# RWKV inverses by blocks of 16 rows with four product stages, and a reordered linear attention, in a two-layer hybrid trunk kernel

## Chip, cores and metric

One core of one Trainium2 chip. The time is device microseconds (us) for one execution of the whole kernel; smaller is better. The engines are PE (TensorE, matrix products; PEld is its weight load), DVE (VectorE), ACT (ScalarE), POOL (GpSimd) and SP (SyncE, which here only issues DMAs). Everything is fp32; a fp32 product appears in the trace as two PE records.

## What is computed

The reference runs two trunk layers over 128 context and 256 latent tokens (384 columns). Each layer has attention, a gated linear attention (GLA) and an RWKV-7 mixer in both directions, then a merge of the three and a feed-forward part. The change touches the GLA and, above all, the RWKV recurrence:

```python
def rwkv7_scan(r, decay, k, v, a_vec, b_vec, s0):
    def step(s, inp):
        rt, wt, kt, vt, at, bt = inp
        sa = jnp.einsum('bhij,bhj->bhi', s, at)
        s = s * wt[:, :, None, :] + sa[..., None] * bt[:, :, None, :] + vt[..., None] * kt[:, :, None, :]
        return s, jnp.einsum('bhij,bhj->bhi', s, rt)
    ...
    y_f, sr_f = rwkv7_scan(r, dec_f, kd_f, vc, -kk, kk * a_f, sr_f0)
    y_b, sr_b = rwkv7_scan(flip_t(r), flip_t(dec_b), flip_t(kd_b), flip_t(vc),
                           flip_t(-kk), flip_t(kk * a_b), sr_b0)
```

## The kernel before

The kernel is written by hand: each engine has its own program, and semaphores join them. A layer has five phases with a barrier between them: projections (0), attention (1), GLA (2), RWKV (3), merge and feed-forward (4). PE products go into six PSUM banks in turn (`item`, `room`): a product waits until the bank used six items earlier has been emptied by the DVE or the ACT. Two more banks serve **fills**. A fill is work of other parts (projections of the gates, `ada`, branch outputs `po`) that PE does in small steps between the steps of its own phase; `fill(k)` does k steps. How many stand at each place of phase 3 is written in the table `FILLS`, one row for each layer (line 349). Steps that are left over are done at the end of the phase (`finish`). The DVE and the ACT empty the fill banks at fixed points of their programs (`side_work`).

Phase 3 takes the 8 RWKV heads as four head pairs n = 0 to 3 (two heads in the partition halves `hr`), each with two directions d and six chunks of 64 tokens. For each pair:

- `logs`, `keys`, `terms` on the DVE, with `decays` and `exps` on the ACT, make the scaled inputs `ar` and `BT`; `grams` (L843) makes the 64x64 strictly triangular matrices `Nt`.
- The inverse of I minus such a matrix is needed. Its 32x32 diagonal blocks are inverted by forward substitution: the DVE turns them into the layout `W` with a stream transpose (`begin`, L2036), the POOL works through 30 rows in 60 dependent operations (L1209, L1211), and the DVE turns the result back twice (`inverses`, L2041 and L2043) and lays it into `ZZ` (L2049).
- `merges` (L856) fills in the block between the diagonal ones by two product stages of 24 small products each: G1 (L863), an ACT copy, G2 (L874, L875), ACT copies into `ZZ`. For the pairs n = 1 and 2 the products of `factors` (MT, BK, VT) and of `turned` (AT, RV) stand between and behind them.
- `transitions` (L949) makes five kinds of `chunkwise` products (WZ, VZ, RT, FT, GG; L946, 24 products each kind), `scan_step` runs the recurrence over the chunks in three steps, and `outputs` makes y.

PE and the DVE go through the pairs in program order. The DVE's order within the round of pair n is: `reads` and `keys`, `transitions`, `terms`, `scan_step` 0 and 1, `logs`, `scan_step` 2, `keys`, `terms`, `grams(n + 2)`, `inverses(n + 1)`; `inverses` waits for the POOL. Before round 0 stands an opening: keys of all heads, head pair 0 and 1's terms, `factors(0)`, `grams(1)` and `inverses(0)`. Below, the time at which WZ of pair n starts on PE is called **T0 to T3**.

Phase 2 (GLA) starts with a chain of decays: z on PE, copies on the ACT (L1413), absolute value on the DVE (L1863), Exp and Ln on the ACT (L1418, L1420), sums on the DVE (L1871 and on), exponentials on the ACT, scaled keys on the DVE (L1893), whose transposes PE waits for (khT, L508). Fourteen distance levels follow (L807), then the outputs `ob` of four heads (L818, L822) and a normalisation, whose last operation is L1967 on the DVE.

## Time and profile before

| what | us |
|---|---|
| median of 3 runs | 2164.12 (2162.21 to 2166.35) |
| the profiled execution | 2163.82 |
| its span, first to last instruction | 2162.0 |
| PE busy | 1946.2 |
| DVE busy | 1020.3 |
| ACT busy | 829.5 |
| POOL busy | 309.5 |

Busy times are unions of the instructions of an engine. Phase 2 stands at 332 to 456 us in layer 0 and 1390.6 to 1515.3 in layer 1; phase 3 at 456 to 742.1 and 1515.3 to 1786. The two phases are repeated nearly alike in the two layers, but layer 0 has more fill work in phase 3.

### The profile page before, as it was taken

How to read it: one execution, taken by the hardware profiler on the slowest of the kernel's cores; microseconds unless marked ns; L12 is line 12 of the kernel's file. 1: busy time of each engine (PE TensorE's matmuls, PEld its weight loads, DVE VectorE, ACT ScalarE, POOL GpSimd, SP SyncE). 2: the span in 40 equal slices, each digit the busy share in tenths (PEclk: the TensorE clock that was granted, in tenths of full speed). 3: DMA queues.
4: the chain of work that ended last, by engine and by line, in shares of the span. 5: the costliest groups of instructions: out<-in, count | busy, mean ns of one | idle time of the engine just before them, and what ended most of it. 6: DMA issues, size and time to landing. Idle time of an engine off the chain costs nothing. (4 is left out here: it accounts for less than half of the span.)

```text
span 2162.0 us, 35730 instructions
## 1 busy us (share of the span) xinstructions
PE 1946.2 (90%) x15251; PEld 1580.7 (73%) x15251; DVE 1020.3 (47%) x1683; ACT 829.5 (38%) x1340; POOL 309.5 (14%) x549
## 2 busy tenths in 40 slices
PE   6899998988689898999989989989786898899998
PEld 3799444655476698999979974546455768899998
DVE  0435425856663454433332454186766545434332
ACT  2433535343353335333253335333433344533321
POOL 2000000007772000000000000000377600000000
PEclk9999999998899999999999999999988899999999
DMA  6543332322103333443434433332200023344442
GB/s 226 175 120 107 104 115 81 97 73 89 50 3 99 129 119 85 131 123 104 131 107 119 127 104 96 105 102 92 70 21 2 3 65 121 97 133 119 116 121 83
DMA packets 267924, 214.31 MB, mean 99 GB/s; under 512 B 7225, under 2 KB 259544, under 8 KB 267512
## 3 DMA queue, kind: packets, MB, share of 16 engines
q1 hardware_dynamic: 264816, 204.43, 31.3%
q0 software_dynamic: 2736, 7.54, 1.1%
q8 instruction: 122, 2.00, 0.4%
q14 instruction: 34, 0.28, 0.0%
q10 hardware_dynamic: 216, 0.06, 0.0%
HBM read 209.13 MB, written 2.88 MB: 98 GB/s over the span
## 5 line engine op out<-in xcount | busy, mean ns | idle before, releaser
L550 PE MATMUL bank<-scr_rounded 128*128 128x384 f32 (+1 forms) x1312 | 444.1, 338 | 0.0
L548 PE MATMUL bank<-scr_rounded 128*128 128x384 f32 x672 | 232.4, 346 | 37.1 <-DVE scr_rounded L1716 35.6
L604 PE MATMUL bank<-h,ring 128*128 128x384 f32 x640 | 238.1, 517 | 29.1 <-DVE gtmp L1703 10.9
L550 PEld LDWEIGHTS bank<-scr_rounded 128*128 128x128 f32 (+1 forms) x1312 | 249.4, 190 | 1.0
L549 PE MATMUL bank<-scr_rounded 128*128 128x384 f32 x672 | 230.4, 343 | 0.0
L1711 DVE TENSOR_TENSOR scr_rounded<-ring,scr_rounded 128x2048 fp32r<-128x2048 f32 (+1 forms) x64 | 136.1, 2126 | 188.4 <-ACT scr_rounded L1266 187.6
L548 PE MATMUL bank<-scr_rounded,gate_rounded 128*128 128x384 f32 (+1 forms) x640 | 214.1, 335 | 4.4 <-DVE scr_rounded L1711 4.4
L549 PE MATMUL bank<-scr_rounded,gate_rounded 128*128 128x384 f32 (+1 forms) x640 | 213.9, 334 | 0.0
L604 PEld LDWEIGHTS bank<-h,ring 128*128 128x128 f32 x640 | 121.2, 198 | 114.8 <-issue 43.4
L599 PE MATMUL bank<-ring,scond 128*2 128x256 f32 x768 | 175.4, 381 | 8.3 <-DVEq L343 5.0
L1711 DVE TENSOR_TENSOR scr_rounded<-ring,gate_rounded 128x2048 fp32r<-128x2048 f32 (+3 forms) x64 | 130.2, 2034 | 104.6 <-ACT gate_rounded L1266 104.0
L1266 ACT ACTIVATE scr_rounded<-ring 128x2048 fp32r<-128x2048 f32 (+1 forms) x64 | 114.0, 1781 | 152.7 <-PE bank L550 75.2
L1266 ACT ACTIVATE gate_rounded<-ring 128x2048 fp32r<-128x2048 f32 (+3 forms) x64 | 109.3, 1707 | 146.5 <-PE bank L550 85.8
L548 PEld LDWEIGHTS bank<-scr_rounded 128*128 128x128 f32 x672 | 130.9, 195 | 42.4 <-issue 38.6
L1211 POOL TENSOR_TENSOR cst<-cst,lora 128x30 f32<-128x30 f32 (+14 forms) x240 | 142.9, 596 | 18.8
L599 PEld LDWEIGHTS bank<-ring,scond 128*2 128x2 f32 x768 | 61.7, 85 | 109.3 <-issue 21.2
L1209 POOL TENSOR_TENSOR lora<-cst 128x30 f32<-128x30 f32 (+14 forms) x240 | 131.9, 550 | 18.2
L549 PEld LDWEIGHTS bank<-scr_rounded 128*128 128x128 f32 x672 | 131.0, 195 | 0.0
L548 PEld LDWEIGHTS bank<-scr_rounded,gate_rounded 128*128 128x128 f32 (+1 forms) x640 | 118.9, 186 | 5.9 <-DVE scr_rounded L1711 5.0
L549 PEld LDWEIGHTS bank<-scr_rounded,gate_rounded 128*128 128x128 f32 (+1 forms) x640 | 118.9, 186 | 1.0
L2241 DVE TENSOR_TENSOR arena<-bank,arena 128x384 f32<-128x384 f32 x44 | 24.5, 558 | 176.7 <-PE bank L550 173.7
L610 PE MATMUL bank<-arena,ring 128*128 128x384 f32 x256 | 90.6, 496 | 4.2 <-DVE gtmp L1703 1.9
(369 smaller groups left out, 3250.1 us busy)
## 6 DMA issues: line engine op xcount, KB each, us to landing
ring<-in_w_in_dram SPq DMA_DIRECT2D x56, 1024.0 KB, 5.3
ring<-in_w_ada_dram SPq DMA_DIRECT2D x48, 1024.0 KB, 5.2
ring<-in_w_ffn_in_dram SPq DMA_DIRECT2D x88, 512.0 KB, 5.1
ring<-in_w_ffn_out_dram SPq DMA_DIRECT2D x32, 704.0 KB, 4.6
ring<-in_w_out_dram SPq DMA_DIRECT2D x8, 1024.0 KB, 5.3
ring<-in_w_po_a_dram SPq DMA_DIRECT2D x4, 1024.0 KB, 6.6
ring<-in_w_po_b_dram SPq DMA_DIRECT2D x4, 1024.0 KB, 5.9
ring<-in_w_po_c_dram SPq DMA_DIRECT2D x4, 1024.0 KB, 5.1
```

What stands on the lines that cost most here:

```text
L548: pe.matmul(o, w_hi[:, k, :], right[0][k], start=k == 0, stop=False)
L549: pe.matmul(o, w_hi[:, k, :], right[1][k], start=False, stop=False)
L550: ins = pe.matmul(o, w_lo[:, k, :], right[0][k], start=False, stop=k == nk - 1)
L599: ins = pe.matmul(b[0:2, 0:256], scond[:, :, k], w[:, k, :], start=k == 0, stop=k == KD - 1)
L604: ins = pe.matmul(b[:, 0:T], w[:, k, 128 * (j % 2):128 * (j % 2) + 128], h[:, k, :], start=k == 0, stop=k == KD - 1)
L610: ins = pe.matmul(b[:, 0:T], w[:, k, 128 * (j % 4):128 * (j % 4) + 128], src[:, k, :], start=k == 0, stop=k == 3)
L1209: gp.tensor_tensor(t, W[:, i + 1:32, i:i + 1].to_broadcast([128, more, i]), over(W[:, i, 0:i], more), mult).then_inc(*step())
L1211: gp.tensor_tensor(W[:, i + 1:32, 0:i], W[:, i + 1:32, 0:i], t, add).then_inc(*(step() if i < 30 else tells("rw_inv")))
L1266: A(shaped(whi[m % 2], name, j), weights(l, name, j), ACT.Copy).then_inc(*tells("w_hi"))
L1711: tt(shaped(wlo[m % 2], name, j), weights(l, name, j), value(shaped(whi[m % 2], name, j)), sub).then_inc(*tells("w_lo"))
L2241: tt(ff[:, j, :], b[:, 0:T], ff[:, j, :], mult).then_inc(*empties("ffi", l, j, 1))
```

## The change

1. **Blocks of 16.** The DVE compresses twice, so that the diagonal blocks are 16x16 (`own`, then `Cc` of 512 columns in place of 1024). `begin` transposes 512 columns. The POOL's 60 operations are gone. `substitution(rows)` on the DVE does rows 1 to 14 in 28 dependent operations of 28 to 112 elements for a partition. For pair 0 it stands in the opening, behind `begin(0)`; for later pairs it is cut into rows 1 to 5, 6 to 10 and 11 to 14, behind `scan_step` 0, 1 and 2.
2. **Four product stages.** With D the inverse of the diagonal blocks and N the part off them, PE makes MM and QQ, then SS, EE and FF, each by `chunkwise`, 24 products for each of the five kinds. ACT copies MM; the DVE copies QQ and adds after SS, EE and FF. The POOL only masks N (`off_blocks`) and lays out the second form of D (`own_blocks`).
3. **Order.** `factors` is split into `factor(n, d)` and `values(n)`, `turned` into `turned` (AT) and `read` (RV); for n = 1 and 2 these stand between the stages. For n = 0 and 3 there are three places for fills in a merge, not one. `FILLS` is new: in layer 0 the steps up to T0 go from 29 to 19, in layer 1 from 27 to 19; the sums of the rows go from 56 to 56 and from 47 to 44. `finish` does what is left.
4. **GLA.** On the ACT the squares of the RWKV keys stand behind Exp and Ln. PE has `fill(4)` before the products of those squares, and `fill(6)` in place of `fill(4)` behind them. The DVE empties only the first two fills before L1871. The `ob` products with `att` are done for all heads first, then those with the states, with the two partition halves in turn.

```diff
-        FILLS = ((4, 6, 2, 4, 4, 4, 2, 2, 1, 1, 1, 1, 1, 2, 1, 1, 1, 1, 2, 1, 1, 1, 2, 2, 2, 2, 1, 1, 1, 1),
-                 (4, 6, 2, 4, 4, 2, 2, 2, 1, 1, 1, 1, 1, 0, 1, 1, 1, 1, 0, 1, 1, 1, 1, 2, 1, 1, 1, 1, 1, 1))
+        FILLS = ((4, 6, 2, 1, 1, 1, 1, 0, 1, 1, 1, 2, 2, 2, 1, 1, 3, 2, 2, 1, 1, 3, 2, 2, 1, 1, 1, 1, 1, 1, 1, 2, 2, 2),
+                 (4, 6, 2, 1, 1, 1, 1, 0, 1, 1, 1, 1, 1, 1, 1, 1, 2, 1, 1, 1, 1, 2, 1, 1, 1, 1, 1, 1, 1, 1, 1, 1, 1, 1))
...
+                    for d in range(2):
+                        chunkwise("MM", "A", n, d, lambda h, c: Zt[d][hr[h], c, :], lambda h, c: Nt[n % 2][hr[h], d, c, :])
+                        chunkwise("QQ", "V", n, d, lambda h, c: Nt[n % 2][hr[h], d, c, :], lambda h, c: Zt[d][hr[h], c, :])
                     if n in (1, 2):
-                        factors(n)
+                        factor(n, 0)
                     else:
                         fill(next(steps))
...
+                        chunkwise("SS", "V", n, d, lambda h, c: Mm[hr[h], d, c, :], lambda h, c: Qm[hr[h], d, c, :])
+                    if n in (1, 2):
+                        factor(n, 1)
+                    else:
+                        fill(next(steps))
...
+                        chunkwise("EE", "V", n, d, lambda h, c: Mm[hr[h], d, c, :], lambda h, c: Sm[d][hr[h], c, :])
...
+                        chunkwise("FF", "V", n, d, lambda h, c: pair[0][hr[h], c, :], lambda h, c: pair[1][hr[h], c, :])
...
+                def substitution(rows):
+
+                    for i in rows:
+                        more = 15 - i
+                        t = term[:, 0:2 * more * i].rearrange("p (j a k) -> p j a k", j=more, a=2)
+                        tt(t, W[:, i + 1:16, :, i:i + 1].to_broadcast([128, more, 2, i]),
+                           W[:, i, :, 0:i].unsqueeze(1).to_broadcast([128, more, 2, i]), mult).then_inc(*step())
+                        dve.wait_ge(*last())
+                        tt(W[:, i + 1:16, :, 0:i], W[:, i + 1:16, :, 0:i], t, add).then_inc(*step())
+                        dve.wait_ge(*last())
...
                     scan_step(n, 0)
+                    if n < 3:
+                        substitution(range(1, 6))
                     scan_step(n, 1)
+                    if n < 3:
+                        substitution(range(6, 11))
...
                     scan_step(n, 2)
+                    if n < 3:
+                        substitution(range(11, 15))
...
-                for hp in range(4):
-                    A(kkn[hp], pc[:, 4 + hp, :], ACT.Square, scale=P(l, "k_k", hp)).then_inc(*tells("rw_kksq"))
                 act.wait_ge(S["gla_abs"], told("gla_abs", l, 1))
...
                 A(lg, lg, ACT.Ln, bias=1.0).then_inc(*tells("gla_log"))
+                for hp in range(4):
+                    A(kkn[hp], pc[:, 4 + hp, :], ACT.Square, scale=P(l, "k_k", hp)).then_inc(*tells("rw_kksq"))
...
+                        pe.matmul(outs_b[hh][:, cs], vbt[:, cc, 128 * hh:128 * hh + 128], att[:, hh, cs], start=cc == 0, stop=cc == 0,
+                                  skip_group_check=True)
+                for hp in range(2):
+                    for cc in range(1, C):
+                        cs = slice(CH * cc, CH * cc + CH)
+                        for d in range(2):
+                            st = s0 if cc == first[d] else s1
+                            for half, r in enumerate(hr):
+                                ins = pe.matmul(outs_b[2 * hp + half][:, cs], st[r, d, hp, :], qe[r, 2 * d + hp, cs], start=False, stop=d == 1,
+                                                skip_group_check=True)
+                    ins.then_inc(psum_ready, 2)
```

PE, phase 3 of layer 0, the merge of pair 1 before. L604 is a fill, L863 is G1, L893 to L916 `factors`, L874 and L875 G2:

```order
L604 MATMUL bank<-h,ring 128x384 x2
L863 MATMUL bank<-scr,cst 32x32 x24
L893 MATMUL bank<-scr 64x128 x12
L508 MATMUL bank<-cst,scr 128x64 x6
L893 MATMUL bank<-scr 64x128 x12
L905 MATMUL bank<-cst,scr 64x64 x12
...
L508 MATMUL bank<-cst,arena 128x128 x3
L916 MATMUL bank<-cst,arena 64x128 x6
L874 MATMUL bank<-scr 32x32
L875 MATMUL bank<-scr 32x32
```

The same place in the changed kernel. L975 is `chunkwise` (twice 12 rows of MM and QQ for each direction, then SS, EE and FF), L915 and L927 are `factor`, L953 AT, L966 RV, L942 the values:

```order
L975 MATMUL bank<-cst,scr 64x64 x12
L975 MATMUL bank<-scr,cst 64x64 x12
...
L915 MATMUL bank<-scr 64x128 x12
L927 MATMUL bank<-cst,scr 64x64 x12
L975 MATMUL bank<-scr,cst 64x64 x24
...
L975 MATMUL bank<-lora,cst 64x64 x12
L975 MATMUL bank<-cst 64x64 x12
...
L942 MATMUL bank<-cst,arena 64x128 x6
L953 MATMUL bank<-cst,scr 64x64 x24
L975 MATMUL bank<-scr,lora 64x64 x12
L975 MATMUL bank<-cst,scr 64x64 x12
L966 MATMUL bank<-arena,gate 64x64 x24
```

The 48 products of 32x32 have become 120 of 64x64, and `factor` and AT stand between the stages. On the DVE, the `inverses` of pair 0 before (L1980 to L1984 are `logs`, L2041 to L2049 the turning back, L2036 `begin` of pair 1, L2064 `reads`):

```order
L1980 SCALAR_TENSOR_TENSOR scr<-cst,arena 128x384
L1982 TENSOR_TENSOR scr<-scr 128x384
L1984 TENSOR_TENSOR scr<-scr,arena 128x384
L2041 STREAM_TRANSPOSE scr<-cst 128x32x32
L2043 STREAM_TRANSPOSE scr<-cst 128x32x32
L2036 STREAM_TRANSPOSE cst<-cst 128x1024
L2049 TENSOR_TENSOR scr<-scr,cst 128x384 x2
L1696 TENSOR_TENSOR mod<-bank,par 128x4
L2064 TENSOR_TENSOR scr<-bank,scr 128x384 x2
```

And in the changed kernel, with L2105 to L2089 the turning back and `begin`, L2160 to L2170 the evictions of QQ, SS, EE and FF:

```order
L2031 TENSOR_TENSOR scr<-scr,arena 128x384
L2105 STREAM_TRANSPOSE scr<-cst 128x16x32
L2110 TENSOR_TENSOR scr<-scr,cst 128x384 x2
L2114 STREAM_TRANSPOSE scr<-cst 128x16x32
L2085 STREAM_TRANSPOSE cst<-cst 128x512
L2089 MEMSET cst 128x16 x2
L2160 COPY scr<-bank 128x384 x2
L2164 TENSOR_TENSOR lora<-bank,scr 128x384
L2164 TENSOR_TENSOR cst<-bank,scr 128x384
...
L2170 TENSOR_TENSOR scr<-bank,scr 128x384 x2
L2129 TENSOR_TENSOR scr<-bank,scr 128x384 x2
```

The DVE no longer waits for the POOL there, and has eight evictions more. Between the scan steps of round 0 (L2149) now stands the substitution (L2097 multiplies, L2100 adds):

```order
L2097 TENSOR_TENSOR lora<-cst 128x100
L2100 TENSOR_TENSOR cst<-cst,lora 128x20x5
L2149 SCALAR_TENSOR_TENSOR scr<-bank,small,scr 128x64 x2
L2097 TENSOR_TENSOR lora<-cst 128x108
L2100 TENSOR_TENSOR cst<-cst,lora 128x18x6
```

Each of the ten operations behind scan step 1 (the last two rows are its first ones) now runs before `logs` and scan step 2 on the DVE.

## Rows read from the trace of the kernel before

**Rows 1.** The page: span, and first row of its busy times.

```profile
span 2162.0 us, 35730 instructions
...
PE 1946.2 (90%) x15251; PEld 1580.7 (73%) x15251; DVE 1020.3 (47%) x1683; ACT 829.5 (38%) x1340; POOL 309.5 (14%) x549
```

**Rows 2.** Windows by stage: length; PE, PEld, DVE, ACT, POOL busy; clock; DMA share, GB/s.

```profile
332.00:456.00 124.00, 112.56 (x736) 69.12 (x737) 84.38 (x164) 51.96 (x79) 1.52 (x2) 0.96 0.31 98
456.00:542.30 86.30, 69.83 (x623) 41.71 (x623) 55.91 (x91) 34.22 (x63) 44.49 (x78) 0.86 0.25 77
542.30:599.90 57.60, 41.44 (x821) 30.76 (x822) 37.36 (x63) 21.23 (x43) 46.34 (x79) 0.88 0.12 39
599.90:644.20 44.30, 37.16 (x809) 29.67 (x804) 31.46 (x57) 21.02 (x43) 29.98 (x56) 0.92 0.01 3
644.20:700.90 56.70, 55.05 (x845) 35.98 (x841) 20.64 (x41) 23.03 (x47) 18.81 (x36) 1.00 0.30 94
700.90:742.10 41.20, 37.89 (x448) 25.48 (x448) 12.81 (x29) 11.31 (x18) 0.87 (x1) 1.00 0.20 59
...
1515.30:1601.10 85.80, 65.98 (x593) 40.94 (x593) 56.86 (x92) 33.44 (x61) 44.63 (x78) 0.86 0.17 53
1601.10:1655.40 54.30, 39.38 (x795) 31.22 (x796) 36.51 (x58) 21.18 (x42) 43.35 (x74) 0.81 0.01 2
1655.40:1704.10 48.70, 36.82 (x800) 29.82 (x794) 32.79 (x57) 19.23 (x41) 34.28 (x62) 0.82 0.01 2
1704.10:1754.80 50.70, 47.47 (x804) 34.26 (x799) 20.60 (x39) 23.70 (x46) 17.28 (x34) 1.00 0.15 44
1754.80:1786.00 31.20, 29.10 (x412) 21.48 (x412) 12.53 (x27) 10.45 (x16) 0.87 (x1) 0.95 0.16 44
```

**Rows 3.** Timeline of PE, layer 0: start, us, group, idle before and its releaser.

```profile
510.50 1.56 PE L893 MATMUL bank<-scr 64*64 64x128 f32 x24 [8.64 <-DVE gate L2101]
...
584.07 2.90 PE L604 MATMUL bank<-h,ring 128*128 128x384 f32 x4 [10.88 <-DVE gtmp L1703]
```

**Rows 4.** PE's waits in total: us, times, longest.

```profile
PE bank L863 <- DVE scr L2049: 27.0, 4, 11.0
```

**Rows 5.** Who waited for the POOL's substitution: us, times.

```profile
  DVE scr L2041: 11.5, 4
```

**Rows 6.** Timeline of PE: G1, a fill step, WZ and VZ together (48 products).

```profile
537.48 0.95 PE L863 MATMUL bank<-scr,arena 32*32 32x32 f32 x48
...
542.25 3.02 PE L946 MATMUL bank<-scr 64*64 64x64 f32 x96 [1.45 <-ACT scr L1569]
...
564.49 1.56 PE L610 MATMUL bank<-arena,ring 128*128 128x384 f32 x4
```

**Rows 7.** Timeline of the DVE: small operations without and with POOL at work, transpose, eviction.

```profile
463.78 0.16 DVE L2009 TENSOR_TENSOR small<-small 128x5 f32<-128x5 f32 x1
...
494.12 0.41 DVE L2009 TENSOR_TENSOR small<-small 128x5 f32<-128x5 f32 x1
...
624.91 1.92 DVE L2041 STREAM_TRANSPOSE scr<-cst 128x1024 f32<-128x1024 f32 x1
...
647.94 1.26 DVE L2064 TENSOR_TENSOR scr<-bank,scr 128x384 f32<-128x384 f32 x2 [7.12 <-PE bank L946]
```

**Rows 8.** Timeline of all engines, phase 2 of layer 0.

```profile
341.62 1.48 ACT L1420 ACTIVATE scr<-scr 128x1536 f32<-128x1536 f32 x1
...
345.20 1.75 DVE L1871 SCALAR_TENSOR_TENSOR scr<-scr 128x1536 f32<-128x1536 f32 x1
...
360.38 1.97 PE L508 MATMUL bank<-cst,scr 128*128 128x128 f32 x8 [9.22 <-DVE scr L1893]
...
431.63 1.61 PE L807 MATMUL bank<-scr 64*128 64x128 f32 x24
...
439.70 0.71 PE L822 MATMUL bank<-scr 64*128 64x128 f32 x4
...
453.09 0.56 DVE L1967 TENSOR_TENSOR arena<-arena 128x384 f32<-128x384 f32 x1
```

More of the change, by code:

```diff
@@ new lines, in merges @@
+                    if n in (1, 2):
+                        values(n)
+                        turned(n)
+                    else:
+                        fill(next(steps))
+                    pe.wait_ge(S["rw_zn"], told("rw_zn", l, n + 1))
+                    for d in range(2):
+                        pe.wait_ge(*emptied("EE", l, n, d))
+                        pair = (Sm[0], Zn[0]) if d == 0 else (Zn[1], Sm[1])
+                        chunkwise("FF", "V", n, d, lambda h, c: pair[0][hr[h], c, :], lambda h, c: pair[1][hr[h], c, :])
@@ L1050, in _ @@
                 turned(0)
+                read(0)
                 fill(next(steps))
@@ L1071, in _ @@
                         fill(next(steps))
-                        factors(3)
+                        factor(3, 0)
+                        factor(3, 1)
+                        values(3)
                         fill(next(steps))
                         turned(3)
+                        read(3)
                         fill(next(steps))
@@ L1602, in _ @@
                 exps(3)
-                factors(0)
+                factor(0, 0)
+                factor(0, 1)
+                values(0)
                 decays(4)
                 turned(0)
+                read(0)
                 for n in range(4):
@@ L1616, in _ @@
                     if n == 2:
-                        factors(3)
+                        factor(3, 0)
+                        factor(3, 1)
+                        values(3)
                         turned(3)
+                        read(3)
                     if n == 2:
@@ L2032, in grams @@
                     dve.wait_ge(*last())
                 def begin(n):
-                    dve.transpose(W, Cc).then_inc(*tells("rw_w"))
+                    dve.transpose(W.rearrange("p j a i -> p j (a i)"), Cc).then_inc(*step())
+                    dve.wait_ge(*last())
+                    flat = W.rearrange("p j a i -> p (j a i)")
+                    for a in range(2):
+                        dve.memset(flat[:, 16 * a:512:33], 1.0).then_inc(*step())
+                    dve.wait_ge(*last())
@@ L2044, in inverses @@
+                    ins.then_inc(*tells("rw_zt"))
+                    dve.transpose(Zc.rearrange("p u j -> p j u"), W.rearrange("p j a i -> p j (a i)")).then_inc(*tells("rw_zc"))
                     dve.wait_ge(*last())
@@ L2090, in scan_step, with merges @@
                                 op0=mult, op1=add).then_inc(*empties("H", l, n, s, d))
-                def factors(n):
-                    i, hp = n % 2, n
-                    for d in range(2):
-                        for j in range(2):
-                            for h in range(2):
-                                side_work("MT", l, n, d, j, h)
-                                dve.wait_ge(psum_ready, filled("MT", l, n, d, j, h))
-                                b = bank("MT", l, n, d, j, h)
-                                tt(MMt[:, d, h, 3 * j:3 * j + 3, :], c3(b[:, 0:T]), over(seen[:, d, :], 3), mult).then_inc(*empties("MT", l, n, d, j, h))
-                    for d in range(2):
-                        c = scanned(d, 0)[1]
-                        ts(HS[:, d, c, :], h0[:, 4 * d + hp, :], es[i][d][:, 0, c:c + 1], None, mult).then_inc(*tells("rw_h"))
+                def merges(n):
+                    for d in range(2):
+                        cp(Qm[:, d, :, :], taken("QQ", n, d)).then_inc(*empties("QQ", l, n, d))
+                    if n in (1, 2):
+                        factor(n, 0)
+                    for d in range(2):
+                        tt(Sm[d], taken("SS", n, d), Qm[:, d, :, :], add).then_inc(*empties("SS", l, n, d))
+                    if n in (1, 2):
+                        factor(n, 1)
+                    for d in range(2):
+                        tt(Sm[d], taken("EE", n, d), Qm[:, d, :, :], add).then_inc(*empties("EE", l, n, d))
+                    for d in range(2):
+                        tt(ZZ[:, d, :, :], taken("FF", n, d), ZZ[:, d, :, :], add).then_inc(*empties("FF", l, n, d))
@@ new lines, in factor @@
+                def factor(n, d):
+                    i, hp = n % 2, n
+                    for j in range(2):
+                        for h in range(2):
+                            side_work("MT", l, n, d, j, h)
+                            dve.wait_ge(psum_ready, filled("MT", l, n, d, j, h))
+                            b = bank("MT", l, n, d, j, h)
+                            tt(MMt[:, d, h, 3 * j:3 * j + 3, :], c3(b[:, 0:T]), over(seen[:, d, :], 3), mult).then_inc(*empties("MT", l, n, d, j, h))
+                    if d:
+                        for e in range(2):
+                            c = scanned(e, 0)[1]
+                            ts(HS[:, e, c, :], h0[:, 4 * e + hp, :], es[i][e][:, 0, c:c + 1], None, mult).then_inc(*tells("rw_h"))
@@ L2147, in _ @@
                 begin(0)
+                substitution(range(1, 15))
                 for g in (2, 3):
@@ L2158, in _ @@
                         logs(6)
[L2159 to L2160 removed]
+                    merges(n)
                     reads(n)
```

236 lines of the change are left out of this document (116 added, 120 removed).

## The prediction

> **What bounds the kernel now.** I read the busy shares first: PE is busy for 1946 of 2162 us, the DVE for less than half, the POOL for a seventh [rows 1]. So PE's order of work is the path, and a change pays where PE stands still or where its work shrinks. Then the windows of the two phases touched [rows 2]. In phase 3 of layer 0 (286 us) PE is busy 70, 41, 37, 55 and 38 us in the opening and the rounds of pairs 0 to 3. 45 us are idle, nearly all before T2; round 2 is full (55.05 of 56.7 us). In layer 1 (271 us) 52 us are idle. The granted clock says that idle time costs twice: it is 0.81 to 0.92 in the stages with stalls and 1.00 in round 2, so behind stalls PE works at 1.2 GHz in place of 2.4 GHz. In window terms (1 - clock) x length, for example 0.14 x 86.3 = 12 us in the opening, is the time at full clock that was lost there.
>
> Which stalls? In the opening PE waits 8.6 us for the eviction of MT, because the DVE is still in the terms of pair 1; in round 0 it waits 10.9 us in a fill whose bank the DVE empties late, behind the inverses [rows 3]. G1 waits for `ZZ` 27 us in four places [rows 4]. But the DVE waited for the POOL only 11.5 us in four places in the whole kernel [rows 5]: the POOL's 41 us for an inverse are mostly hidden. What it costs beside that is contention. A DVE operation of 5 elements takes 0.16 us when the POOL rests and 0.41 us when it works [rows 7].
>
> **Part 1, the substitution.** 28 dependent operations of 28 to 112 elements, 2240 in all. From the row of 5 elements 0.16 us [rows 7], from an eviction of two times 384 elements 1.26 us, 0.63 for each [rows 7]: a fixed part near 0.16 and about 1.2 ns for an element. 28 x 0.16 + 2240 x 0.0012 = 7.2 us; with a few hundredths for each dependence I take **8 us** an inverse. Bounds: 28 x 0.16 = 4.5 us below and 28 x 0.41 = 11.5 us above, the row with contention. I stay near the lower row since the POOL now has only three short operations for a pair.
>
> The row says that a small operation is nearly all fixed cost. The Trainium skill, VectorE: DVE Perf Modes, section on the TRN2 errata, says the same in kind and speaks against cutting work into small operations; its table gives 58 cycles and one for each element at 0.96 GHz. By that table, an estimate, an inverse would be 28 x 60 ns + 2.3 = 4.0 us, and the six inverses behind the opening and the first loops would make the sum some 20 us smaller; I go by the row.
>
> **Part 2, the DVE's path in a round.** From T0 to G1's input before: 571.7 - 542.3 = 29 us of evictions, keys, terms and `grams`, then POOL wait, two transposes of 1.92 us [rows 7], one for the next pair and the layout, 39 us in sum. After: the same 29 us less 6 us (some 15 operations of 384 elements fall from about 0.9 to 0.56 us as the contention of rows 7 goes) plus 8 us for the substitution, 1.5 us for the second compression, and half a transpose and the layout, 2 us: 33.5 us in round 0 and 33 in round 1, where before it was 39 and 31. So the DVE is earlier by 5 us in round 0 and later by 2 in round 1. It is this path that PE waits for, not a POOL.
>
> **Part 3, the merge on PE.** WZ and VZ, 48 products of 64x64, take 3.02 us [rows 6], so 24 take 1.5 us, and five kinds take 7.5 us. G1 takes 0.95 us [rows 6] and G2 about 0.5. **+6 us for each pair**, 48 us of PE for the 8 pairs. The stages themselves: in each, the DVE needs 0.63 us for a direction while PE does the other, so with `factor` or a fill between them there is little wait. A merge that had 4.8 us from G1 to T0 (with one fill step and 1.45 us of waiting, rows 6) becomes 3.0 + 1.5 + 1.5 + 1.5 + 0.7 and three steps of 1.5 to 1.9 us: 13.5 us. In rounds 0 and 1 with `factor`, AT, RV and VT in it: 3 + 4.5 + 3.3 x 2 + 1.5 + 1.5 + 1.5 = 18.6 us behind the DVE's signal, 20 in round 0 where `logs` delays the first eviction.
>
> **Part 4, stage by stage** (before from rows 2).
> - Opening, 86 us. The DVE has 8 us more and 6 less contention before it empties MT, so PE leaves its stall about 1 us later; `ZZ` is ready 8 us earlier, and the merge is 9 us longer: **+0.5**. But 10 fill steps (8 in layer 1) of about 1.5 us [rows 6] have left the opening and must be done later: PE stands idle for some 35 us there in place of 17.
> - Round 0: 33.6 + 20 = **54 us** against 57.6 and 54.3. The stall of 10.9 us goes, but its place is taken by the merge.
> - Round 1: 33 + 18.6 = **51.5 us** against 44.3 and 48.7.
> - Round 2: PE is full, so all work adds: 56.7 + 8.9 for the merge of pair 3 with its two more fill steps = **66 us**, and 50.7 + 7.3 = **58 us**.
> - Round 3: three fill steps more, 4.4 us, less a little stall: **45 us** against 41.2, and **35 us** against 31.2.
>
> Layer 0: 86.5 + 54 + 51.5 + 66 + 45 = 303 against 286, **+17 us**. Layer 1: 86.5 + 54 + 51.5 + 58 + 35 = 285 against 271, **+14 us**.
>
> **Part 5, GLA.** Here I see a gain. Ln ends at 343.1, but L1871 starts at 345.2, since the DVE first empties fills; and Exp starts behind the four squares and a table load, 1.3 us after it could [rows 8]. Both go: the scaled keys are 2.8 us earlier, and so is khT. PE waits 9.2 us there [rows 8], and two fill steps more fit into the wait. The 16 state products of `ob` take 0.71 us for each two (four records), 5.6 us; when two partition halves alternate, as in L807, 24 records take 1.6 us [rows 8], so 32 take 2.1: 3.2 us less of PE, and 2.6 less on the way to the last L1967, which ends at 453.7 [rows 8]. The phase ends at 456.0 because PE then has two `ada` fills left; one of them has moved to the front. New end about 451.3 - 2.8: **-7.5 us a layer**, -15 in all. If the tail doesn't follow, only the 2.8 at the front and 2.2 of the tail remain, -10; nothing makes it a loss.
>
> **Sum.** 17 + 14 - 15 = +16 us on 2163.8 of the profiled execution (0.3 below the median of the runs), so **2180 us**.
>
> **Rivals.**
> - *PE's work alone sets the rounds.* If the DVE's path is shorter than I sum it (substitution at 4.5 us, evictions under PE), the rounds shrink to PE's work at full clock. Layer 0 behind the opening: 286 - 86 = 200 us, less 28 idle and some 8 of clock, plus 18 of merges and 15 of fills: 197, so -2 with the opening. Layer 1: 185, less 31 and 18, plus 18 and 12: 166, so -18; I allow it -10 with the stalls that its few fills leave. With GLA: -27, **2137 us**; halfway, 2150. For it: the DVE is busy only 31 of 44 us in round 1. Against it: those are dependent steps, and 8 us are added to them. It decides from a substitution under 5 us.
> - *The two parts cancel.* The rounds cost half of what I say, **2164 us**.
> - *The GLA part doesn't act*, because the fill work moved forward is missed by no one and the DVE's tail holds the end: +31 less 2, **2193 us**.
> - *The substitution runs at the row with contention*, 11.5 us: 3.5 us more in three places a layer, **2201 us**. For it: `W` is read in short runs, and the POOL masks at that time.
>
> **Numbers.** Forecast (2170 to 2190) 0.52; PE's work alone 0.24; cancelling 0.12; GLA without effect 0.07; slow substitution 0.05. Measurement tells apart about 0.2%, 4 us. Faster 0.25, same 0.13, slower 0.62. The range takes in half of the first rival and the last but one: 2147 to 2196 us.
>
> **What would show it.** In the changed profile: L2097 and L2100 at 0.2 to 0.3 us each and 8 us an inverse; L975 at 1.5 us for 24 products; T1 - T0 near 54, T2 - T1 near 51; PE idle over 30 us in the opening; round 2 at 66 and 58 us with clock 1.00; phase 2 at 116 to 118 us. I am wrong if the opening is shorter by over 5 us, or if rounds 0 and 1 are under 50 us.

## The result, and the profile after it

The changed kernel takes **2175.81 us** (median of 7 runs, 2173.01 to 2179.07); the kernel before, in the same rounds, 2166.35 us (2162.21 to 2170.43). The ratio is 1.0046, with a 95% interval of 1.0031 to 1.0061: **slower by 9.5 us**. The interval leaves out 1, but the difference is under half a percent. The forecast was 2180 us.

The page of the changed kernel, its first rows, as in [rows 1]:

```profile
span 2176.9 us, 37908 instructions
...
PE 1974.6 (91%) x16403; PEld 1608.5 (74%) x16403; DVE 1064.2 (49%) x1995; ACT 820.0 (38%) x1308; POOL 58.4 (3%) x85
```

PE is busy for 28 us more, the DVE for 44 us more, and 251 us of the POOL's work are gone. Which stage pays, the windows show. They have the columns of [rows 2]; the first six are phase 2, the opening and the rounds 0 to 3 of layer 0, the others the same of layer 1:

```profile
335.16:447.48 112.32, 105.18 (x737) 63.97 (x737) 84.02 (x164) 51.35 (x79) 1.52 (x2) 1.00 0.35 114
447.48:536.59 89.11, 64.36 (x703) 43.33 (x703) 58.56 (x129) 31.64 (x56) 6.00 (x6) 0.79 0.03 8
536.59:586.85 50.26, 45.36 (x964) 34.75 (x964) 40.47 (x100) 20.96 (x40) 3.17 (x3) 1.00 0.26 86
586.85:646.80 59.95, 49.93 (x989) 36.55 (x987) 38.71 (x100) 19.44 (x40) 3.17 (x3) 0.91 0.17 55
646.80:711.03 64.23, 62.27 (x991) 43.71 (x987) 30.46 (x77) 23.09 (x43) 1.70 (x2) 1.00 0.17 52
711.03:757.84 46.81, 43.44 (x476) 27.78 (x474) 13.53 (x31) 11.69 (x19) 0.87 (x1) 1.00 0.32 95
1407.29:1519.61 112.32, 105.18 (x737) 63.97 (x737) 84.02 (x164) 51.40 (x79) 1.52 (x2) 1.00 0.36 115
1519.61:1608.49 88.88, 64.14 (x704) 43.28 (x704) 58.56 (x129) 31.64 (x56) 6.00 (x6) 0.79 0.03 8
1608.49:1658.80 50.31, 41.71 (x941) 34.09 (x941) 40.48 (x100) 20.40 (x39) 3.17 (x3) 0.97 0.20 65
1658.80:1708.55 49.75, 41.51 (x951) 34.42 (x949) 38.09 (x96) 20.10 (x39) 3.17 (x3) 0.97 0.01 3
1708.55:1769.32 60.77, 56.64 (x962) 41.61 (x956) 30.31 (x76) 20.47 (x39) 1.70 (x2) 1.00 0.12 37
1769.32:1802.41 33.09, 31.65 (x426) 22.14 (x424) 13.08 (x28) 12.23 (x18) 0.87 (x1) 1.00 0.15 41
```

Against [rows 2]:

| stage | layer 0: before, after, forecast | layer 1: before, after, forecast |
|---|---|---|
| phase 2 | 124.0, 112.3, 116.5 | 124.7, 112.3, 117 |
| opening | 86.3, 89.1, 86.5 | 85.8, 88.9, 86.5 |
| round 0 | 57.6, 50.3, 54 | 54.3, 50.3, 54 |
| round 1 | 44.3, 60.0, 51.5 | 48.7, 49.8, 51.5 |
| round 2 | 56.7, 64.2, 66 | 50.7, 60.8, 58 |
| round 3 | 41.2, 46.8, 45 | 31.2, 33.1, 35 |

Phase 2 gives back 24 us in sum; phase 3 costs 24 us in layer 0 and 12 in layer 1. The remaining 3 us of the profiled span lie ahead of phase 2 of layer 0, where the code is the same; in the runs below phase 2 of layer 0 starts anywhere from 331.6 to 334.8 us, here at 335.2, so I don't put them down to the change.

Three readings behind the table. First, the substitution on the DVE; the groups (busy time, mean ns of one) and operations of round 0 of layer 0:

```profile
L2097 DVE TENSOR_TENSOR lora<-cst 128x28 f32<-128x28 f32 (+6 forms) x112 | 27.9, 249 | 3.2
L2100 DVE TENSOR_TENSOR cst<-cst,lora 128x28 f32<-128x28 f32 (+6 forms) x112 | 27.3, 244 | 3.9
...
549.34 0.21 DVE L2100 TENSOR_TENSOR cst<-cst,lora 128x28 f32<-128x28 f32 x1
...
553.09 0.28 DVE L2100 TENSOR_TENSOR cst<-cst,lora 128x112 f32<-128x112 f32 x1
```

224 operations at 0.25 us, and 0.03 to 0.05 us between them: 8 inverses of 8 us, on a chain of the DVE at whose end PE waits.

Second, stalls: PE's two in the opening of layer 0, and in its round 1 two of PE and one of the ACT (columns of [rows 3]):

```profile
494.33 1.56 PE L915 MATMUL bank<-scr 64*64 64x128 f32 x24 [12.20 <-ACT arena L1523]
...
503.87 1.56 PE L915 MATMUL bank<-scr 64*64 64x128 f32 x24 [6.70 <-DVE gate L2180]
...
598.41 5.30 PE L606 MATMUL bank<-ring,scond 128*2 128x256 f32 x16 [2.17 <-ACT modrow L1294]
...
615.55 4.58 PE L617 MATMUL bank<-arena,ring 128*128 128x384 f32 x8 [5.02 <-ACT modrow L1294]
...
613.45 0.21 ACT L1537 ACTIVATE small<-scr 128x6 f32<-128x6 f32 x1 [5.51 <-DVE scr L2031]
```

The single stall of 8.64 us at MT has become 19 us in two pieces: few fills are left to stand there. In round 1 the fills wait twice for a bank that the ACT empties late, once within the three steps in front of scan step 0 and once behind scan step 2, and what stands behind the waits runs more slowly: 5.30 us for 16 records of L606 that take 3.62 us elsewhere, 4.58 us for 8 of L617 that take 2.82 us at the upper clock level (2.4 GHz). The second wait goes back to the DVE: ten operations of the substitution stand ahead of `logs` (L2031), the ACT waits 5.51 us for `logs`, and only behind the exponentials does it empty the bank.

Third, phase 2, where [rows 8] showed khT behind 9.22 us of idleness:

```profile
360.68 1.09 PE L515 MATMUL bank<-cst,scr 128*128 128x128 f32 x8 [2.42 <-DVE scr L1940]
361.70 1.97 PE L800 MATMUL bank<-gate,scr 128*64 128x128 f32 x32
...
433.72 2.06 PE L833 MATMUL bank<-scr 64*128 64x128 f32 x32
```

### The profile page after: what moved, and what is told of

Its sections match the earlier page's. It is cut to its first block, busy times and chain, and to the rows that moved or that the text cites. A ratio compares the mean times of both kernels' runs of the same rounds, so it can differ in the third digit from the quotient of the medians.

```text
span 2176.9 us, 37908 instructions
## 1 busy us (share of the span) xinstructions
PE 1974.6 (91%) x16403; PEld 1608.5 (74%) x16403; DVE 1064.2 (49%) x1995; ACT 820.0 (38%) x1308; POOL 58.4 (3%) x85
## 4 chain that ended last, share of the span: by engine, by line
PE 74%; DVE 12%; ACT 8%; issue 2%; DMA 1%; PEldq 1%; PEld 0%; ACTq 0%; POOL 0%; DVEq 0%; SPq 0%; POOLq 0%
PE bank L555 11%; PE bank L557 11%; PE bank L556 11%; PE bank L611 7%; PE bank L606 6%; PE bank L975 5%; PE bank L1159 3%; PE bank L1161 3%; PE bank L1160 3%; PE bank L617 2%; PE bank L515 2%; PE bank L814 2%; ACT h L1324 1%; DVE cst L2100 1%; DVE lora L2097 1%
## 5 line engine op out<-in xcount | busy, mean ns | idle before, releaser
L611 PE MATMUL bank<-h,ring 128*128 128x384 f32 x640 | 232.7, 507 | 14.2 <-ACT gtmp L1307 8.0
L606 PE MATMUL bank<-ring,scond 128*2 128x256 f32 x768 | 180.0, 388 | 9.7 <-DVEq L350 5.0
L606 PEld LDWEIGHTS bank<-ring,scond 128*2 128x2 f32 x768 | 62.5, 86 | 114.9 <-issue 29.9
L617 PE MATMUL bank<-arena,ring 128*128 128x384 f32 x256 | 96.1, 519 | 11.9 <-DVEq L350 5.3
L617 PEld LDWEIGHTS bank<-arena,ring 128*128 128x128 f32 x256 | 48.5, 198 | 43.9 <-issue 17.8
L915 PE MATMUL bank<-scr 64*64 64x128 f32 x768 | 33.5, 304 | 38.7 <-ACT arena L1523 24.4
```

The costliest lines, as they stand in the source:

```text
L606: ins = pe.matmul(b[0:2, 0:256], scond[:, :, k], w[:, k, :], start=k == 0, stop=k == KD - 1)
L611: ins = pe.matmul(b[:, 0:T], w[:, k, 128 * (j % 2):128 * (j % 2) + 128], h[:, k, :], start=k == 0, stop=k == KD - 1)
L617: ins = pe.matmul(b[:, 0:T], w[:, k, 128 * (j % 4):128 * (j % 4) + 128], src[:, k, :], start=k == 0, stop=k == 3)
```

## Experiments

Each run is given by its ratio to the kernel before on the same chip; the changed kernel stands at 1.0046. A hundredth is 21.7 us.

### The two parts apart

The GLA part alone, on the kernel before, and the RWKV part alone:

```diff
-                fill(4)
+                fill(6)
...
-                for hp in range(4):
-                    A(kkn[hp], pc[:, 4 + hp, :], ACT.Square, scale=P(l, "k_k", hp)).then_inc(*tells("rw_kksq"))
                 act.wait_ge(S["gla_abs"], told("gla_abs", l, 1))
```

> The kernel before with the GLA part of the change alone (ACT squares behind Exp and Ln, fill(4) ahead of and fill(6) behind the products of the squares, the DVE's later fill evictions, the regrouped ob products); the inverses are the old ones. Theory W (the windows of the changed kernel are the whole of it: phase 2 takes 112.3 us there in place of 124.0 and 124.7, and nothing comes back later): 24 us less than the kernel before, near 2142 us. Theory P (the prediction's terms, 7.5 us a layer): near 2151 us. Theory N (the gain in phase 2 needs the new phase 3, or is given back by the fill work that phase 3 no longer finds): 2160 us or more.

Measured: **2143.39 us** (2142.88 to 2145.68), ratio 0.9904 (0.9891 to 0.9918), 21 us less. Both phases 2 have the length of the changed kernel:

```profile
334.12:446.42 112.30, 105.18 (x737) 63.97 (x737) 83.98 (x164) 51.33 (x79) 1.52 (x2) 1.00 0.36 115
```

> The changed kernel with the GLA part put back as it was; only the inverses, their order and the table of fills are new. If the two parts are independent, this is the changed kernel plus what the GLA part gives: near 2200 us by the windows (phase 3 is 24 us longer in layer 0 and 12 in layer 1), near 2191 us by the prediction's 15 us. If they are not independent, the sum of this run's difference and that of the GLA part alone differs from the difference of the changed kernel (about +10 us) by more than 4 us.

Measured: **2197.0 us** (2196.21 to 2198.08), ratio 1.015 (1.0136 to 1.0164), 33 us more. -21 and +33 make +12; the changed kernel is at about +10. Within the noise the parts are independent, and theories P and N of the first run are out: P is 8 us off, N 17.

The front of the GLA part alone, on the kernel before (order on the ACT, fills and their evictions, but the old `ob` products):

> The kernel before with only the front of the GLA part (ACT squares behind Exp and Ln, fill(4) and fill(6), the DVE's later fill evictions); the ob products stay as they were. Together with the ob products the gain was 21 us. By the windows of the changed kernel, khT starts 2.8 us earlier, and no stall of 9.2 us stands ahead of it, so that the 32 products behind it take 1.97 us in place of 3.68; one ada step has left the end. I expect 5.5 to 8 us a layer from the front and 4 from the tail: 2149 to 2155 us. Rival (the tail holds the end of the phase, as the prediction had it, so the front alone gives only 2.8 us a layer): 2158 us or more.

Measured: **2153.0 us** (2151.92 to 2156.23), ratio 0.9944 (0.9928 to 0.9961), 12 to 14 us less. So the front gives some 6.5 us a layer and the tail 4 to 5. The rival, 2.8 us a layer, falls.

### What the substitution costs on the DVE

```diff
                     scan_step(n, 0)
-                    if n < 3:
-                        substitution(range(1, 6))
                     scan_step(n, 1)
-                    if n < 3:
-                        substitution(range(6, 11))
...
                     scan_step(n, 2)
-                    if n < 3:
-                        substitution(range(11, 15))
```

> The changed kernel without the substitution behind the scan steps (pairs 1 to 3 get wrong inverses; pair 0 keeps its own); the DVE's path is 8 us shorter in each round, PE's work is the same. Theory D (the DVE's path sets rounds 0 and 1): each of these four rounds shrinks until PE's own work fills it, that is by 5 us in layer 0 and by 8 in layer 1 (PE is busy 45.4 of 50.3 us in round 0, 41.6 of 50 us in layer 1), in sum 20 to 26 us less than the changed kernel, near 2153 us; round 2 stays. Rival PE (PE's own work sets the rounds and the DVE is waited for only at its edges): less than 6 us, 2170 us or more.

Measured: 2147.17 us (2146.13 to 2151.1), ratio 0.9924 (0.9911 to 0.9938): **26 us less than the changed kernel**. Rounds 0 and 1 of layer 1, which were 50.31 and 49.75 us:

```profile
1593.30:1636.30 43.00, 40.02 (x941) 32.71 (x941) 33.65 (x72) 20.39 (x39) 3.17 (x3) 1.00 0.23 76
1636.30:1679.30 43.00, 39.64 (x951) 32.71 (x949) 31.41 (x68) 20.10 (x39) 3.17 (x3) 1.00 0.01 3
```

7 of 8 us come back from each, PE's busy time falls by 2 us with the clock at its upper level throughout, and round 2 gives 2 to 3.5 us. In layer 0, which has more fills, round 0 falls only from 50.26 to 46.45 us, where PE is then busy for 44.95, and round 1 from 59.95 to 53.30. The DVE's chain sets these rounds as the change left them; the rival, that PE's own work sets them, falls, though in round 0 of layer 0 PE's work is the next limit, after 4 us.

Its place: all 28 operations in one piece behind scan step 2.

> The changed kernel with all 28 operations of a substitution in one piece behind scan step 2, not cut in three behind the three scan steps. Theory L (the DVE's path is one chain, and its length does not depend on the place): within 4 us of the changed kernel, 2172 to 2180 us. Rival W (the pieces behind scan steps 0 and 1 stand partly in time that the DVE waits for the next scan product of PE, so late ones cost more): 2 to 3 us in each of the four rounds 0 and 1, 2184 us or more. Rival Q (the pieces delay the scan's next step, so together behind it they cost less): 2168 us or less.

Measured: 2181.63 us (2180.3 to 2182.81), ratio 1.0073 (1.0058 to 1.0088), some 6 us above the changed kernel, between theory L and rival W; the intervals of the two ratios touch. What is late then are the keys and terms of the next pair, in round 0 and, through a fill's bank, in round 1:

```profile
562.03 1.55 PE L865 MATMUL bank<-scr 64*64 64x64 f32 x24 [4.32 <-DVE scr L2063]
...
623.86 2.90 PE L611 MATMUL bank<-h,ring 128*128 128x384 f32 x4 [7.39 <-DVE gtmp L1749]
```

Cutting it in three is worth a little; where it stands is not what costs most. But its place decides one wait. The fill behind scan step 2 in round 1 of layer 0, which waited 5.02 us for the ACT, in the run without the substitution and then in this one:

```profile
605.35 2.82 PE L617 MATMUL bank<-arena,ring 128*128 128x384 f32 x8 [0.45 <-ACT modrow L1294]
...
610.59 2.82 PE L617 MATMUL bank<-arena,ring 128*128 128x384 f32 x8 [0.46 <-ACT modrow L1294]
```

Both have the changed kernel's table of fills. So this wait is not one of too many fills alone; it is the substitution's, since it holds up `logs` and with it the ACT. The first wait stays, at 1.81 us in both (2.17 in the changed kernel).

### One product stage

```diff
-                    for d in range(2):
-                        pe.wait_ge(*emptied("SS", l, n, d))
-                        chunkwise("EE", "V", n, d, lambda h, c: Mm[hr[h], d, c, :], lambda h, c: Sm[d][hr[h], c, :])
...
-                    for d in range(2):
-                        tt(Sm[d], taken("EE", n, d), Qm[:, d, :, :], add).then_inc(*empties("EE", l, n, d))
```

> The changed kernel without the stage EE (24 products of 64x64 for a pair and two DVE additions; the inverses are incomplete). Theory M (a stage lies on the path from the DVE's transposes to T, in all 8 merges; 1.5 us of PE and, where no work is left to stand between, some of the DVE's additions): 1.5 to 2 us for each pair, 12 to 16 us less than the changed kernel, 2160 to 2164 us. Rival S (the stages hide in other stalls): under 8 us, 2168 us or more.

Measured: 2164.84 us (2161.95 to 2169.84), ratio 0.9997 (0.9983 to 1.0012): 11 us less than the changed kernel, 1.3 us for each of 8 merges. Theory M is a little high, rival S too low. The 24 products are 1.5 us of PE, so a stage costs about its products and no long wait.

### The fills that left the opening

```diff
-        FILLS = ((4, 6, 2, 1, 1, 1, 1, 0, 1, 1, 1, 2, 2, 2, 1, 1, 3, 2, 2, 1, 1, 3, 2, 2, 1, ...
+        FILLS = ((4, 6, 2, 4, 4, 4, 2, 0, 1, 1, 1, 1, 1, 1, 1, 1, 1, 1, 1, 1, 1, 2, 1, 1, 1, ...
```

The row of layer 1 changes in the same way: seven steps more in its opening, fewer in rounds 1 to 3.

> The changed kernel with another table of fills: in layer 0 ten steps more in the opening (places 4 to 7: 4, 4, 4, 2 in place of 1, 1, 1, 1) and ten fewer in rounds 0 to 2; in layer 1 seven more in the opening and some fewer at the end. Theory F (PE stands idle for 25 us in each opening, and waits there for the DVE, so fills are free there, while round 2 is full and round 1 of layer 0 waits 7 us for the ACT in its three bunched fills): opening unchanged within 3 us, layer 0 shorter by 10 to 15 us, layer 1 by 5, in sum 2158 to 2164 us. Theory D (the fills push MT and with it the whole chain of the opening): the opening grows by what the rounds lose, 2173 to 2180 us.

Measured: **2157.63 us** (2155.21 to 2162.01), ratio 0.9972 (0.9961 to 0.9983): 16 us less than the changed kernel, and less than the kernel before. Opening, rounds 0 to 2 of layer 0:

```profile
446.71:535.27 88.56, 74.59 (x765) 45.49 (x765) 60.49 (x132) 33.19 (x59) 6.70 (x6) 0.90 0.20 67
535.27:587.70 52.43, 45.38 (x979) 36.57 (x979) 40.75 (x103) 20.85 (x41) 3.17 (x3) 0.93 0.14 43
587.70:636.30 48.60, 40.03 (x925) 33.26 (x924) 37.06 (x94) 19.85 (x38) 3.16 (x3) 0.96 0.01 3
636.30:698.10 61.80, 58.40 (x979) 41.42 (x975) 30.57 (x77) 21.27 (x41) 1.70 (x2) 1.00 0.18 55
```

The opening takes ten more steps in 0.5 us less: they stood in waiting time. Round 1, with four steps fewer (6.2 us) and without the waits for the ACT, falls from 59.95 to 48.60; the run doesn't part the two. Round 0 shows the other side: with three steps fewer it is 2.2 us longer. PE is busy as long as before (45.38 us) at a clock of 0.93, and stands idle for 7.1 us in place of 4.9, the longest time (3.46 us) before the outputs (L1024). Theory F holds.

### What the POOL's substitution had cost

The kernel before, with 58 of the 60 POOL operations of each inverse left out:

```diff
-                    for i in range(1, 31):
+                    for i in range(30, 31):
```

> The kernel before with 58 of the 60 POOL operations of each substitution left out (the inverses are wrong; PE, ACT and DVE do what they did). It prices what the change took away. Theory C (the POOL was mostly hidden but slowed the DVE: 6 us of contention in each of some six stages, and 11.5 us of waits): 25 to 40 us less than the kernel before, 2125 to 2140 us, with 384-element DVE operations at 0.55 us throughout. Rival H (hidden work costs nothing): at most the 11.5 us that the DVE waited, 2153 us or more.

Measured: **2110.11 us** (2106.88 to 2120.79), ratio 0.9748 (0.9714 to 0.9782): 47 to 62 us less, more than theory C. Opening and round 0 of layer 0, then of layer 1:

```profile
457.76:537.99 80.23, 69.04 (x621) 41.24 (x622) 50.19 (x91) 34.26 (x63) 4.12 (x8) 0.89 0.26 82
537.99:587.10 49.11, 41.74 (x820) 31.32 (x821) 31.10 (x63) 21.21 (x43) 0.92 (x3) 0.86 0.15 45
...
1500.39:1573.70 73.31, 61.87 (x593) 38.41 (x593) 51.05 (x92) 33.49 (x61) 4.14 (x8) 0.91 0.20 62
1573.70:1615.50 41.80, 35.20 (x795) 28.42 (x796) 29.53 (x58) 21.21 (x42) 0.92 (x3) 0.92 0.01 2
```

They were 86.3, 57.6, 85.8 and 54.3 us (the profile is of the slowest of the four executions, 10 us above the median). The DVE's busy time in them falls by 5.7, 6.3, 5.8 and 7.0 us, the contention that the prediction priced at 6. But the stages fall by 6, 8.5, 12.5 and 12.5 us. What can add to the contention is the wait in `inverses` and the clock behind the stalls (0.86, 0.88, 0.86 and 0.81 before, 0.89, 0.86, 0.91 and 0.92 here); their shares were not measured apart. The POOL, busy 14% of the span and waited for 11.5 us, cost some 50.

Which operations contend? The kernel before, round 0 of layer 0, the POOL at work; the last row is the changed kernel, where the POOL rests:

```profile
549.68 1.01 DVE L2070 TENSOR_TENSOR scr<-bank,cst 128x384 f32<-128x384 f32 x2
...
551.72 1.05 POOL L1211 TENSOR_TENSOR cst<-cst,lora 128x238 f32<-128x238 f32 x1
...
552.18 1.01 DVE L2005 TENSOR_TENSOR scr<-scr,arena 128x384 f32<-128x384 f32 x1
...
554.00 0.60 DVE L2009 TENSOR_TENSOR small<-small 128x5 f32<-128x5 f32 x1
...
545.49 0.55 DVE L2052 TENSOR_TENSOR scr<-scr,arena 128x384 f32<-128x384 f32 x1
```

The first row is two operations in 1.01 us, with one input in PSUM (`bank`), as long as the same two take in the changed kernel. L2005 is one operation with both inputs in SBUF, the memory of the tiles that are not banks: 1.01 us, where the changed kernel has 0.55. The POOL suffers too: its operation in the second row takes 1.05 us, and the same one of 238 elements takes 0.65 at 557.00. The Trainium skill, SBUF — State Buffer, section "SBUF: two separate sides", says so: a DVE operation with two SBUF inputs and a POOL operation that reads SBUF exclude each other for a whole instruction. The rows agree: both engines' operations with SBUF inputs grow, the DVE's with a PSUM input don't.

### The same 28 operations on the POOL

If the POOL cost 50 us because 41 us of its work reached over the DVE's keys and terms, a short chain that stands beside the merge, where the DVE takes from PSUM, should cost next to nothing. (The expectation on record is more careful; it allows up to 10 us of contention.)

```diff
+                def substitution(n):
+
+                    gp.wait_ge(S["rw_w"], told("rw_w", l, n + 1))
+                    for i in range(1, 15):
...
                     own_blocks(n)
+                    if n < 3:
+                        substitution(n + 1)
...
                 def inverses(n):
 
+                    dve.wait_ge(S["rw_inv"], told("rw_inv", l, n + 1))
```

> The changed kernel with the same 28 operations of each substitution moved from the DVE to the POOL (all four pairs), in one piece behind begin; everything else as in the changed kernel. Leaving the substitution out gave 2147 us. The POOL needs about 14 us for it (operations of 58 to 108 elements took 0.39 to 0.46 us on the POOL before), of some 45 us that it has. Theory V (the DVE's 8 us are the cost, contention is smaller): 2147 plus up to 10 us of contention, minus the 8 us of pair 0 in each opening that are saved too: 2140 to 2157 us. Rival K (contention and the hand-over cost as much as the move saves, as the change seems to assume): 2165 us or more.

Measured: **2133.7 us** (2133.18 to 2137.32), ratio 0.9853 (0.9825 to 0.9881), 42 us less than the changed kernel; the time lies below the expected range. Rounds 0 and 1 of layer 1, then the POOL's first and last operation of an inverse and the DVE beside it and behind it (layer 0):

```profile
1581.10:1624.10 43.00, 40.01 (x940) 32.69 (x942) 33.71 (x72) 20.39 (x39) 14.27 (x37) 1.00 0.23 76
1624.10:1667.10 43.00, 39.65 (x951) 32.71 (x949) 31.40 (x68) 20.08 (x39) 13.22 (x33) 1.00 0.01 3
...
520.53 0.28 POOL L1264 TENSOR_TENSOR lora<-cst 128x28 f32<-128x28 f32 x1
...
532.07 0.24 POOL L1267 TENSOR_TENSOR cst<-cst,lora 128x28 f32<-128x28 f32 x1
...
526.21 0.56 DVE L2174 TENSOR_TENSOR lora<-bank,scr 128x384 f32<-128x384 f32 x1 [1.78 <-PE bank L975]
...
538.75 0.55 DVE L2068 TENSOR_TENSOR scr<-scr,arena 128x384 f32<-128x384 f32 x1
...
539.69 0.16 DVE L2072 TENSOR_TENSOR small<-small 128x5 f32<-128x5 f32 x1
```

These rounds have the length that they have with no substitution at all; in layer 0 they differ from it by 0.05 and 0.2 us. The POOL needs 11.8 us beside evictions, and is done before the DVE's keys begin (534.80).

The products of the substitution done three times, so that the POOL works twice as long:

> As pool16 (2133.7 us), with each product of the substitution done three times into the same place, so that the POOL has 56 operations for an inverse, near 26 us in place of 13; nothing else changes. Theory K (the POOL's work costs nothing while it lies beside the merge, where the DVE only evicts, and costs when it reaches the DVE's keys and terms, where a 5-element operation took 0.41 to 0.60 us beside the POOL and 0.16 us without): 10 to 20 us more, 2144 to 2154 us, and 5-element operations of 0.3 us or more in rounds 0 and 1, which are 0.16 us in pool16. Rival H (what cost time before was only the length of the POOL's chain, 41 us, for which the DVE waited in the end): within 4 us of pool16, since 26 us still end long before they are waited for.

Measured: 2138.7 us (2132.28 to 2142.57), ratio 0.9872 (0.9849 to 0.9894): 4 us above pool16, which its interval doesn't separate from zero. The stages say more. Rounds 0 and 1 of layer 1, which were 43.00 each:

```profile
1584.10:1629.50 45.40, 41.57 (x939) 33.36 (x941) 34.68 (x72) 20.40 (x39) 26.57 (x63) 0.96 0.22 72
1629.50:1674.30 44.80, 41.30 (x953) 34.34 (x949) 32.17 (x68) 20.16 (x39) 26.66 (x64) 0.96 0.01 3
```

The DVE is busy 0.8 to 1.0 us longer, its 5-element operation in the first terms of each round takes 0.27 to 0.31 us while the second stays at 0.16, and the rounds grow by 2.4 and 1.8 us. That is theory K's mechanism at a third of its price or less; in layer 0, where more fills fill the rounds, it makes +1.0 and -1.2 us.

With the fill table of the run above:

> As pool16, with the table of fills of the run that moved fill steps into the opening (that gave 18 us on the changed kernel). Theory: the two gains add, since one shortens the DVE's path in the rounds and the other fills idle time in the opening: 12 to 18 us under pool16. Rival: with the DVE out of the opening's path PE has less idle time to fill there, and the rounds are full again: under 8 us. It beats the kernel before with the GLA part alone (2143 us) if it comes under 2139.

Measured: **2114.14 us** (2110.79 to 2115.76), ratio 0.9756 (0.9733 to 0.978), 21 us under pool16, more than the 12 to 18 expected: the gains add. Opening and rounds 0 and 1 of layer 0:

```profile
444.18:530.50 86.32, 75.63 (x765) 47.25 (x765) 55.91 (x104) 32.97 (x59) 29.94 (x57) 0.90 0.22 70
530.50:575.10 44.60, 41.86 (x974) 33.30 (x973) 34.19 (x75) 20.82 (x40) 14.01 (x36) 1.00 0.16 50
575.10:616.80 41.70, 38.41 (x931) 31.84 (x926) 30.35 (x66) 19.88 (x38) 13.01 (x32) 1.00 0.01 3
```

Two more steps between the halves of the opening's factor, taken from round 2:

```diff
                 factor(0, 0)
+                fill(2)
                 factor(0, 1)
```

> As pool16_refill (2114.1 us), with two fill steps of round 2, which is full (PE busy 58.24 of 58.4 us), moved into the stall of 5.4 us between the two halves of the opening's factor, in each layer. Theory: 2 x 1.5 us less in each layer, and less work at half clock behind the stall, 2106 to 2110 us. Rival (the fills push the second half of factor and with it T0): no change, 2112 to 2117 us.

Measured: **2111.39 us** (2107.63 to 2112.97), ratio 0.9746 (0.9732 to 0.9761). The opening of layer 0 falls from 86.3 to 83.6 us, but rounds 0 and 1 grow by 2 us each; the intervals overlap, and the difference is not settled: the time lies above the theory's range and below the rival's. Both kernels leave nothing of the computation out; they are 2.5% faster than the kernel before and 1.5% faster than that with the GLA part alone.

## Why the prediction was right, step by step

**Part 1, the substitution: right.** 8 us forecast; in the opening it runs from 479.16 to 487.3 us, and leaving it out gives 7 us in rounds 0 and 1 of layer 1. The table of the Trainium skill (VectorE: DVE Perf Modes, section on the TRN2 errata), by which an inverse would be an estimated 4.0 us, doesn't agree: an operation of 112 elements takes 0.28 us, not 0.18. The same section of the Trainium skill also has a formula for a fp32 tensor_tensor of N elements, (N + 151)/0.96 ns, which the prediction passed over; it does agree, with 0.27 us for 112 elements and an estimated 6.7 us an inverse, where the operations measure 6.9.

**Part 2, the DVE's path: right in round 0.** MM starts 33.5 us behind T0 in layer 0 (570.05 - 536.59) and in layer 1. The forecast has the same figure by a slip: its own terms, 29 - 6 + 8 + 1.5 + 2, make 34.5. In round 1 of layer 1 it is 33.5 for 33. In round 1 of layer 0 MM starts 43.7 us behind T1, not 33: the fills in front of it wait 2.17 and 5.02 us for the ACT, and what follows runs in part at half clock.

**Part 3, the merge: right, a little high.** 13.6 us in pair 0, where 13.5 stood, 16.8 and 16.3 in pairs 1 and 2, where 20 and 18.6 stood; DVE and PE wait for each other less than I summed. A stage is 1.3 to 1.5 us.

**Part 4, the stages: the sum short by 5 us** (+36 for +31). Here steps failed:
- *Opening, +0.5*: it is +3. PE leaves the stall at MT 1.9 us later in layer 0 and 2.4 in layer 1, for 1. `ZZ` was to be ready 8 us earlier and the merge to be 9 us longer, which by itself makes +1 and not +0.5; the merge starts 4.5 to 6 us earlier and is 8 to 9 us longer. PE's idle time is 25 us, where the forecast had 35 and, as a sign, over 30; the clock is 0.79, not 0.86. How much of the 3 us is the clock was not measured apart.
- *Round 1 of layer 0, 51.5*: it is 60.0, the largest miss. The round was summed from the DVE's path and the merge, with fills as mere length, and the ACT's path was missing. The ACT empties the fills' banks behind its exponentials, which wait for `logs`, and `logs` waits for ten operations of the substitution. Without the substitution there the wait of 5.02 us is 0.45 and the round 53.3 us; with fewer fills in the round and others, in the run with the other table, both waits are gone and the round is 48.6. So that wait needs both, the substitution ahead of `logs` and the fills at that place.
- *Rounds 0, 54*: 50.3, since the merge takes 16.8 us and not 20.
- *Round 2*: at clock 1.00, as forecast, 64.2 and 60.8 us for 66 and 58; full in layer 0, with 4 us idle in layer 1.
- *The signs*: an opening shorter by over 5 us didn't come. Rounds 0 and 1 under 50 us did in one place, by a hair: 49.75 us in round 1 of layer 1, beside 50.26, 50.31 and 59.95.

**Part 5, GLA: right in kind, short by 9 us** (-24 in the trace for -15; -21 in the run of that part alone). khT is 2.8 us earlier, as forecast. A term was missing for what the stall does behind itself: in place of 9.22 us PE waits 2.42, and behind that khT takes 1.09 us and not 1.97, L800 (L793 before) 1.97 and not 3.68, the next `ada` fill 3.62 and not 3.95; 2.9 us in sum, with the window's clock at 1.00 in place of 0.96. The prediction charges this to the stalls of phase 3, and forgot it here. The `ob` products take 5.2 us where they took 9.3, so 4.1 us less on the way to the end, not 2.6. The last 1.9 us are what is left over; they fit the `ada` fill that no longer ends behind the DVE (before, PE's last fill product started 1.7 us behind the end of L1967, now it starts before that end), but no run shows them alone.

So two errors of opposite sign, +5 and -9, left the total 4 us under the forecast. That it came so near is in part luck: phase 3 of layer 0 was 7 us over its forecast, that of layer 1 2 us under, and the GLA part 9 under. The side was right for reasons that were given: PE has some 6 us more for each pair, the DVE has 8 us more for each inverse on a chain that PE waits for, and fills have left the opening's waits. The last reason alone decides the side: with the other table of fills the changed kernel is 6 us faster than the kernel before.

**The rivals.** PE's work alone: refuted by the run without the substitution. Cancelling and GLA without effect: refuted by the two parts apart, with +33 and -21 us. The contended rate: refuted, the operations take 0.25 us.

**What it did not see** is the size of what the change removed. The text has the POOL "mostly hidden", with 6 us of contention a stage. The 6 us are right; the cost of the POOL, 47 to 62 us, isn't in any term of its own, though it is in the stage lengths through the shorter DVE path. The parts as far as they were measured: POOL chain away -47 to -62, substitution on the DVE in place of a short one on the POOL +42, the table of fills in place of the other one +16, one of the stages +11. If they simply add, the RWKV part at +33 leaves 11 to 26 us for the other stages and the second compression. That remainder was not measured by itself.

## What to carry over

A helper engine with little busy time can cost far more than the wait for it shows, here some 50 us for 11.5 us of waiting: price it by running the kernel without its work. Before moving its work to the engine on the critical path, shorten it and place it where that engine reads PSUM. And count fill work by the stall that it stands in: a step moved out of waiting time into a full stage costs its whole length, and the stall that it leaves can cost half clock behind it. Work put ahead of an operation that a third engine waits for can stop the first one by a bank: follow the chain through all engines, not only through the two that were changed.

## What was not expected of the hardware

- Contention of DVE and POOL depends on the DVE's operands: 0.55 us became 1.01 with two SBUF inputs, a pair of operations with one PSUM input stayed at 1.01 us. It acts on both sides: the POOL's first operations of 28 elements took 0.92 and 0.56 us beside the DVE's `logs` in the opening, and 0.28 and 0.26 us beside evictions (the POOL's spans in a profile are rough).
- In the rounds of layer 1, 12 us of POOL work for an inverse cost nothing that can be measured, and twice as many operations cost about 2 us each; the old chain of 41 us cost 12.5 us in round 0 and 4.4 in round 1.
- PE idle for 9.22 us in phase 2 ran at half clock behind it and lost 2.9 us more; idle for 2.42 us there it lost none. The length of the idle time alone doesn't decide: in round 1 of layer 0 2.17 us of it were followed by 5.30 us of work that takes 3.62 at the upper level.
